# A 1-core kernel of three transformer layers: a raw ring of 8 slots in place of 10, and five split weight buffers in place of four

## The reference, cut to what matters

```python
def ada_modulate(x, c, norm_g, ada_w, ada_b):
    ada = jax.nn.silu(c) @ ada_w + ada_b                 # 1024 x 3072 weights for one vector
    shift, scale, gate = jnp.split(ada, 3, axis=-1)
    h = rmsnorm(x, norm_g) * (1.0 + scale[:, None, :]) + shift[:, None, :]
    return h, gate[:, None, :]

def even_layer(...):
    h, gate_res = ada_modulate(x, c, norm_g, ada_w, ada_b)
    a, u, v, gate = _split(h @ in_w, EVEN_SIZES)
    ...
    return x + gate_res * (y @ out_w)

def second_block(...):
    mod = c_act @ w_mod[l] + b_mod[l]                    # 1024 x 9216 weights for one vector
    ...
    x = x + 0.5 * g1[:, None, :] * swiglu(h, ffn1_w_gate[l], ffn1_w_up[l], ffn1_w_down[l])
```

## Time and profile before

| what | us |
|---|---|
| median of 3 runs | 989.41 (989.23 to 990.48) |
| the profiled execution | 992.07 |
| its span, first to last instruction | 990.3 |
| TensorE busy | 954.0 |
| VectorE busy | 714.2 |
| ScalarE busy | 507.6 |
| loaded from memory | 217.25 MB, 220 GB/s over the span |

### The profile page before, as it was taken

One profiled execution on the slowest core, in us unless ns is written; L12 is line 12 of the kernel. 1 busy time (PEld: TensorE's weight loads), 2 busy tenths in 40 slices (PEclk: granted clock), 3 DMA queues, 4 the chain that ended last, 5 costly groups with the idle time before them and its releaser, 6 DMA issues.

```text
span 990.3 us, 17238 instructions
## 1 busy us (share of the span) xinstructions
PE 954.0 (96%) x7025; PEld 876.7 (89%) x7025; DVE 714.2 (72%) x994; ACT 507.6 (51%) x745; POOL 41.8 (4%) x68
## 2 busy tenths in 40 slices
PE   6999999999999999999999999999999999999998
PEld 6799999989799789999778888889998978898987
DVE  4778877767866766576899988977988765465554
ACT  4654364456544446544755456474646454444444
POOL 2100000000000003320100000000000000000000
PEclk9999999999999999999999999999999999999999
DMA  9987586844875894658378887776534457474731
GB/s 363 384 279 257 184 290 234 297 167 150 273 248 183 287 302 153 234 214 300 84 242 270 292 276 251 265 251 216 153 124 126 153 170 234 149 262 143 253 110 43
DMA packets 134247, 219.43 MB, mean 222 GB/s; under 512 B 8585, under 2 KB 100090, under 8 KB 134168
## 3 DMA queue, kind: packets, MB, share of 16 engines
q1 hardware_dynamic: 132416, 214.99, 64.9%
q0 software_dynamic: 992, 1.76, 0.7%
q10 hardware_dynamic: 760, 1.59, 0.4%
HBM read 217.25 MB, written 1.05 MB: 220 GB/s over the span
## 4 chain that ended last, share of the span: by engine, by line
PE 75%; DVE 11%; DMA 6%; issue 4%; ACT 4%; SPq 0%; ACTq 0%; DVEq 0%
PE pw L569 50%; PE pacc L569 24%; DMA ring<-in_odd_in_w 3%; DVE ACC L1676 3%; DVE WL L1660 2%; ACT WH L1175 1%; ACT AR L1175 1%; DMA ring<-in_ada_w 1%; DVE SQT L1756 1%; DVE hl L1761 1%; PE pw L1022 1%; DMA ring<-in_odd_out_w 1%; DMA ring<-in_ffn_w_down 1%; ACT hh L1175 1%; DMA cst<-in_consts 1%
## 5 line engine op out<-in xcount | busy, mean ns | idle before, releaser
L1175 ACT ACTIVATE WH<-ring 128x1024 fp32r<-128x1024 f32 x288 | 302.6, 1057 | 300.1 <-PE pw L569 125.0
L1660 DVE TENSOR_TENSOR WL<-ring,WH 128x1024 fp32r<-128x1024 f32 x288 | 348.0, 1224 | 90.8 <-ACT WH L1175 90.1
L569 PE MATMUL pacc<-YH,WH 128*128 128x256 f32 x672 | 192.9, 287 | 2.6 <-issue 1.7
L569 PE MATMUL pw<-hh,WH 128*128 128x256 f32 x704 | 187.8, 288 | 4.4 <-ACT AR L1175 2.1
L569 PE MATMUL pacc<-YH,WL 128*128 128x256 f32 x672 | 190.1, 283 | 0.0
L569 PE MATMUL pacc<-YL,WH 128*128 128x256 f32 x672 | 190.1, 283 | 0.0
L569 PE MATMUL pw<-hh,WL 128*128 128x256 f32 x704 | 184.9, 284 | 0.0
L569 PE MATMUL pw<-WH,hh 128*128 128x512 f32 x448 | 177.0, 395 | 4.4 <-DVE WL L1660 4.0
L569 PE MATMUL pw<-WL,hh 128*128 128x512 f32 x448 | 174.9, 390 | 0.0
L569 PEld LDWEIGHTS pw<-hh,WH 128*128 128x128 f32 x704 | 135.7, 193 | 9.2 <-issue 6.3
L569 PE MATMUL pw<-hl,WH 128*128 128x256 f32 x704 | 142.7, 284 | 0.0
(11 more groups left out here) (272 smaller groups left out, 782.2 us busy)
## 6 DMA issues: line engine op xcount, KB each, us to landing
ring<-in_w_mod SPq DMA_DIRECT2D x72, 512.0 KB, 5.6
ring<-in_odd_in_w SPq DMA_DIRECT2D x56, 512.0 KB, 6.0
ring<-in_ada_w SPq DMA_DIRECT2D x48, 512.0 KB, 6.8
ring<-in_ffn_w_gate SPq DMA_DIRECT2D x88, 256.0 KB, 3.6
ring<-in_ffn_w_up SPq DMA_DIRECT2D x88, 256.0 KB, 4.5
ring<-in_ffn_w_down SPq DMA_DIRECT2D x44, 512.0 KB, 5.1
ring<-in_even_in_w SPq DMA_DIRECT2D x40, 512.0 KB, 7.4
ring<-in_even_out_w SPq DMA_DIRECT2D x16, 512.0 KB, 6.4
```

Source lines behind the costliest of these rows:

```text
L569: return eng.matmul(o, a, b, start=start, stop=stop, skip_group_check=True)
L1175: return eng.activation(dst, src, func, **kw)
L1660: tt(WL[:, i % NL, :], slot(half_of(i)), WH[:, i % NH, :].bitcast(F32), SUB).then_inc(s_lo, 1)
```

## The change

Three constants. The ring shrinks by two slots, and each of the split buffers grows by one, so that the memory they take together is the same (18 slots of 4 KB per partition). ScalarE and VectorE split one piece further ahead.

```diff
--- before.py
+++ after.py
@@ -22,9 +22,9 @@
-RING = 10
-NH, NL = 4, 4
-AHEAD_H, AHEAD_L = 3, 2
+RING = 8
+NH, NL = 5, 5
+AHEAD_H, AHEAD_L = 4, 3
```

## The result

The changed kernel takes 1357.28 us (median of 4 runs, 1353.95 to 1359.85), the kernel before beside it 989.89 us (989.23 to 990.48). The ratio is 1.371 (95% interval 1.368 to 1.374). That is 367.4 us more, where the forecast said 287; the time lies inside the stated range of 1175 to 1420.

A forecast was written before the change was run, and what follows sets the result against it. TensorE, busy 96% of the span, was taken to bound the kernel. Woven stretches +331, cushion -34, hidden work against detour -10 gave +287; 992.1 + 287 = 1279, less 2.7 for the median: 1276 us, range 1175 to 1420.

The forecast's parts named there:

- Placement: In the four woven stretches, 44 ada units' 88 halves are each followed directly by the low part needing their slot.
- Price of one: VectorE's stand from an ada half's end to the low part, through load and high part: 5.07 us, landing taken as 3.8.
- Bounds of 3.3 and 5.6 us: Landing times of the ring loads used for the outer cases: 1172 us at 3.3, 1434 us at 5.6.
- Raw sum: VectorE's busy time plus exposures against the four woven stretches' lengths: +37.9, +34.5, +125.1 and +133.6, together +331 us.
- Cushion: At the head of each of the four stretches, three pieces in hand come off the sum: 34 us, leaving +297.
- Hidden side work against the detour: Up to 35 us of VectorE's other work hides in exposures; ScalarE's queued evacuations cost some 25 places about 1 us: net -10.
- The start: Eight loads go out at once in place of ten; the queue should not run dry: between 0 and 2 us.
- The rest unchanged: The stretches behind 655 us and the opening were to keep their length.
- (a): Rival, faster: exposures fit under the five buffers, only TensorE's 5.7 us of waits for low parts go: 984 us; 3%.
- (c): Rival: same loop with TensorE's clock falling at the gaps, 1396 us if all at half speed; 13% for above 1330.
- (d): Rival: ring loads land as slowly as in the loaded queue, 5.6 us: 1434 us; 6%.
- What would show it: Signs: VectorE's waits for high parts about 400 us, TensorE's for low parts over 250, loads waiting for ada sums.

The follow-up runs named there:

- ada_first: The changed kernel with VectorE reading each step's ada half ahead of that step's low part instead of behind it: 1106.56 us, ratio 1.117.
- ada_two_units_early: The changed kernel with VectorE reading each woven ada unit two main units earlier: 985.42 us, ratio 0.996 to the kernel before.
- less_tensor_work: The changed kernel without the third product (weights' high part by activations' low part) in the input projections and the FFN's up projections: 1309.74 us.
- ada_one_unit_early: The changed kernel with VectorE reading each woven ada unit one main unit earlier: 990.19 us, ratio 1.0006 to the kernel before.

## Why the prediction was right, and where not

**Placement.** That 88 ada halves are each followed directly by the low part that needs their slot: right. Taking away this succession and nothing else (ada_first) brought back 251 us, moving it a unit apart all 367.

**Price of one, 5.07 us.** Right. Median of the time from the end of an ada half to the low part behind it 5.5, 6.0, 5.05 and 4.97 us in the four stretches, mean 5.48. The landing taken as 3.8 us was 4.3 in the turn shown, but over the 88 loads behind an ada half 3.4 to 5.0, median 3.7 and mean 3.8. The Trainium skill's fit (DMA: Bandwidth & Descriptors, "Anatomy of one DMA — SWDGE (gpsimd) path"), by which I had estimated 3.2 us, is for DMAs issued from gpsimd, and these loads are issued by the sync engine. It is 0.5 us below the median measured here; by it the result would have been further off. Bounds of 3.3 and 5.6 us held it.

**Raw sum, +331 us.** Right, in part by luck: +337. By stretch 37.9, 34.5, 125.1 and 133.6 were forecast, and 25.2, 38.3, 142.4 and 131.4 came. The sum over VectorE's order also closes by itself: the times behind the ada halves grew by 460.7 - 84.6 = 376 us, and the rest of VectorE's order took 39 us less. The luck is that two things left out of the raw sum nearly cancel. It added the exposures to all of VectorE's work, while 57 us of that work lie inside them; and it let VectorE never stand elsewhere, while 49 of its 458 us of idle time in these stretches (843.9 less 385.6 busy) lie outside them.

**Cushion, -34 us.** This step failed. I took three pieces in hand at the head of each stretch off the sum. Nothing of the kind is in the measured lengths, and the intervals behind the stretches grew by 21 us in all where I had them unchanged. It may be that what a stretch uses up of the pieces in hand is missing in the interval behind it. That is argued, not shown: I didn't follow it piece by piece.

**Hidden side work against the detour, net -10 us.** Also too good. Of the 461 us behind the ada halves 300 are idle time directly before the low part; the other 161 are some 57 us of other work, where I had hidden up to 35, and waits for other things, ScalarE's evacuations among them. But the detour by ScalarE's queue, which I had put at 25 us, was undervalued: the high parts' extra depth alone cost 60.5 us, through evacuations queued behind late high parts, and in the kernel after TensorE waits 61.1 us for ScalarE's evacuations where it had waited 5.8. How much of the 60.5 is still separate once low parts stand directly behind their ada halves can't be read from these runs.

**The start, 0 to 2 us.** 2.4 us (54.0 for 51.6).

**The rest unchanged.** Right for the last third (325.6 for 324.7 us), wrong by 21 us for the intervals.

So the 362 us that the span grew, for 287, are made up of these: cushion 34, net 10, raw sum 6, start and intervals 24, last third 1. The other 5.5 us up to 367 come from the profiled executions, 3.3 us below the median after and 2.2 us above the median before.

**The rivals.** (a), faster by depth alone, didn't come about, but its term of 5.7 us was real: ada_two_units_early won 5.0 of it. (c), the clock: it fell to between 0.81 and 0.85 in the stretches. In the turn shown TensorE stood 3.23 us up to 93.89, and the granted clock at 94 to 96 was 0.50. The rule of the Trainium skill (TensorE: Matmul & The Clock Gate, "HAM oscillation — how this bites in real kernels") agrees with that for this gap. But less_tensor_work shows that the lower clock cost nothing there. The reason given against (c) was only half of it: the clock did come back between the gaps (a mean of 0.81 to 0.85, not 0.50), but the gaps didn't vanish (271 of the 843.9 us of the stretches are idle on TensorE), and so TensorE had time to spare. (d), landing at 5.6 us, wasn't the case for the loads behind an ada half (5.0 at most). The result lies halfway between the forecast's 1276 and the 1434 of (d), but what fills that half is mostly the cushion (34 us) and the start and intervals (24), not the landing.

**What would show it.** VectorE's waits for high parts grew to 400.7 where 400 was said; the loads wait for ada sums; the load engines' share fell; the loads behind an ada half landed in 3.7 us, though the median of all w_mod loads on the page rose (6.2 for 5.6). One sign was wrong: TensorE's waits for low parts are 64 us and not over 250. TensorE lost the time, but most of its waits end with something else in the same queues. The sign should have been TensorE's idle time as a whole (302.6 us of the span), or VectorE's.

## What to carry to other kernels

In a ring, count how far the read that frees a slot stands from the first operation that needs the load into it, on each engine that needs it; that distance, rather than the number of slots, is the time that the load has, and splitting further ahead takes from it. Here the same eight slots cost nothing measurable with two steps to ScalarE's high part and three to five of VectorE's operations to the low part, 7.7% with one step and two or three operations, 12 to 14% with no step and two or three operations, and 37% with no step and one operation. When a depth is bought with slots, move the reads that free slots forward by as much as the depth has moved the consumers.

## What I had not expected

Low parts one further ahead, which brings the distance to one, cost three times as much (+231.5 us) as the ring of eight slots itself (+75.6), which had brought it from four or more to two or three, since two loads that had overlapped in 38 of 44 pairs then follow one another in all of them.

High parts one piece further ahead, at no cost in buffers, slowed ring 8 by 60.5 us and ring 9 by 37.3, by their place ahead of evacuations in ScalarE's queue. In ada_one_unit_early, where the loads are issued earlier, the whole kernel takes 990.2 us at the same depth, so little room is left for such a cost.

The granted clock can fall to 0.71 (mean of an 88 us stretch, less_tensor_work) with no effect on the length of that stretch, where TensorE isn't the bound; the clock was here a sign of waiting, not a cause.
